# Expert weights of a sparse-attention and mixture-of-experts step: two of the six ring slots of an expert released half by half and loaded as halves of 1 MB

## What is computed

```python
logits = (x @ w_router) + b_router
top_v, top_e = lax.top_k(logits, 4)          # 4 of 32 experts for each row
gates = jax.nn.softmax(top_v, axis=-1)
...
gu = xe @ w_gu[e] + b_gu[e]                  # 1024 x 2048 weights
gate = jnp.minimum(gu[:, :1024], 7.0)
up = jnp.clip(gu[:, 1024:], -7.0, 7.0)
act = (up + 1.0) * gate * jax.nn.sigmoid(1.702 * gate)
y[rows] += gates[rows] * (act @ w_down[e] + b_down[e])   # 1024 x 1024 weights
...
y_prompt, y_sample = rms_norm(x + y, g_final)
```

## Time and profile before

| | us |
|---|---|
| median of 3 runs | 1653.48 |
| lowest, highest | 1653.24, 1654.1 |
| the profiled execution | 1653.29 |
| its span, first to last instruction | 1651.8 |
| TensorE matmuls busy | 1615.7 (98%) |
| VectorE, ScalarE, GpSimd busy | 609.4, 302.4, 204.7 |
| moved by DMA | 510.01 MB, 309 GB/s over the span |

### The profile page before, as it was taken

How to read it: one execution, slowest core, us unless ns; L and a number is a source line. 1 busy time by engine, 2 the same in 40 slices (tenths; PEclk the granted TensorE clock), 3 DMA queues, 4 the chain that set the end, 5 groups by cost and what they waited for, 6 DMA issues and landing times. The chain is left out here.

```text
span 1651.8 us, 33511 instructions
## 1 busy us (share of the span) xinstructions
PE 1615.7 (98%) x13818; PEld 763.7 (46%) x13818; DVE 609.4 (37%) x1186; ACT 302.4 (18%) x618; POOL 204.7 (12%) x267
## 2 busy tenths in 40 slices
PE   9999999999998999999999999999999999999996
PEld 7677587786745333333333333333333333333332
DVE  4359549403315333323233233323333233323333
ACT  1310120017112111112111211121111211111112
POOL 3624300015000010000000000000000000000000
PEclk9999999999998899999999999999999999999996
DMA  7456646621454699999999999999999999999963
GB/s 239 145 171 215 230 150 217 214 76 74 172 205 158 229 397 395 392 401 398 393 395 390 402 389 400 386 399 395 392 390 396 399 392 403 386 398 395 398 261 114
DMA packets 70505, 510.01 MB, mean 309 GB/s; under 512 B 11310, under 2 KB 11758, under 8 KB 45230
## 3 DMA queue, kind: packets, MB, share of 16 engines
q1 hardware_dynamic: 60070, 485.28, 74.0%
q0 software_dynamic: 10384, 24.06, 6.2%
HBM read 491.61 MB, written 22.37 MB: 311 GB/s over the span
## 5 line engine op out<-in xcount | busy, mean ns | idle before, releaser
L1209 PE MATMUL PS<-weight_ring,region_experts 128*32 128x512 f32 x6144 | 680.2, 594 | 2.6 <-issue 1.7
L1209 PEld LDWEIGHTS PS<-weight_ring,region_experts 128*32 128x32 f32 x6144 | 200.5, 110 | 413.3 <-issue 410.4
L1216 PE MATMUL PS<-weight_ring,act_turned 128*32 128x512 f32 x2048 | 232.2, 594 | 0.0
L834 PE MATMUL PS<-region_x,region_w 128*128 128x260 f32 (+1 forms) x928 | 209.4, 385 | 0.9 <-DVE region_x L1415 0.9
L834 PEld LDWEIGHTS PS<-region_x,region_w 128*128 128x128 f32 x928 | 175.2, 190 | 31.8 <-issue 3.4
L1536 DVE TENSOR_TENSOR region_experts<-region_experts,region_x 128x640 bf16<-128x640 f32 x33 | 27.2, 825 | 402.0 <-DMA region_experts<-b_gu 402.0
L1216 PEld LDWEIGHTS PS<-weight_ring,act_turned 128*32 128x32 f32 x2048 | 63.3, 110 | 137.7 <-issue 134.0
L616 POOL DMA_INDIRECT y_acc<-region_x,idx_i x32 | 46.9, 1465 | 641.5 <-issue 641.5
L1222 PE MATMUL PS<-weight_ring,act_turned 128*32 128x256 f32 x2048 | 122.2, 379 | 0.0
L1222 PEld LDWEIGHTS PS<-weight_ring,act_turned 128*32 128x32 f32 x2048 | 66.6, 110 | 71.2 <-issue 38.3
L600 POOL DMA_INDIRECT region_x<-h_rows,idx_i x33 | 33.5, 1014 | 431.8 <-DVE idx_i L1551 352.3
(11 more groups left out here) (266 smaller groups left out, 1301.8 us busy)
## 6 DMA issues: line engine op xcount, KB each, us to landing
weight_ring<-w_gu SPq DMA_DIRECT2D x128, 2048.0 KB, 13.8
weight_ring<-w_down SPq DMA_DIRECT2D x64, 2048.0 KB, 16.6
region_w<-w_mt SPq DMA_DIRECT2D x33, 512.0 KB, 4.4
weight_ring<-cache_kT SPq DMA_DIRECT2D x64, 256.0 KB, 4.0
weight_ring<-cache_v SPq DMA_DIRECT2D x64, 256.0 KB, 4.0
weight_ring<-w_out SPq DMA_DIRECT2D x2, 2048.0 KB, 10.7
weight_ring<-bias_strip SPq DMA_DIRECT2D x1, 2560.0 KB, 13.1
region_x<-xT SPq DMA_DIRECT2D x4, 536.0 KB, 7.0
```

The source lines that it names most:

```text
L834: mm = pe.matmul(PB[j % 2][:, a, 0:width], lhs(k), rhs(k)[:, width * a:width * a + width], start=(k == 0), stop=(k == nk - 1))
L1209: mm = pe.matmul(out[GRP * j:GRP * j + GRP], hTe[:, k, GRP * g:GRP * g + GRP], weights(c)[:, k, :], start=(k == 0), stop=(k == KD - 1))
L1216: pe.matmul(bank(3)[GRP * j:GRP * j + GRP], actT[:, k, GRP * g:GRP * g + GRP], w_dn[:, k, 512 * q:512 * q + 512], start=(k == 0), stop=(k ...
```

## The change

In the expert loop SyncE no longer loads c1 and c3 whole after round 3. The first halves of both (k = 0 to 3, 8 KB of each partition) are loaded once TensorE has done steps 0 to 3 of round 3, for which there is a new semaphore, `third_half`; the second halves are loaded after the round, as the whole slots were. Both halves of a slot count up the slot's semaphore, so TensorE waits for 32 per expert in place of 16. The loads of expert 0 ahead of the loop are cut in the same way, with nothing else between the halves. For the signal, TensorE's call of steps 0 to 5 of round 3 is split into 0 to 3 and 4 to 5.

```diff
@@ -288,7 +288,7 @@
         hTe_ready h_done hfT_ready hfT_taken hf_done idx_ready kidx_in kinew_set kvu late_in lgp_done lgs_done
         log_taken m_done m_ready mask_done mb_done mb_ready mq_done mxT_ready nmax_s og_ready om_done ones_set
         out_done po_step pool_done pool_may pool_pad proj_done psT_ready ps_norm pt_ready pt_taken ptz_done
-        pv_pair rank_ready relu_done rms_set round_done router_ready row_ms rsumT_ready rsum_set s_ready
+        pv_pair rank_ready relu_done rms_set round_done third_half router_ready row_ms rsumT_ready rsum_set s_ready
         sel_ready sidx_taken sig_done slot5_set slot_ready slots_moved small_in smask_done sq_done sq_sum
         ss_ready stT_in strip_in sums_ready turned unused_done up_full vnew_in vtail_out warm_set wblk_done
         wcol_in wiT_in wi_out wo0_in wo1_in wv_in xg_done xn_in xt_ready y_ready zero_late zero_rows zi_set
@@ -420,6 +420,12 @@
                     src = w_down[bass.ds(e, 1), c - 4].rearrange("a p x -> (a p) x")
                 sp.dma_start(W6[:, slot(c):slot(c + 1)], src).then_inc(r_full[c], 16)
 
+            def half_load(c, z, e):
+
+                src = w_gu[bass.ds(e, 1), c].rearrange("a p x -> (a p) x")
+                at = RING // 2 * z
+                sp.dma_start(W6[:, slot(c) + at:slot(c) + at + RING // 2], src[:, at:at + RING // 2]).then_inc(r_full[c], 16)
+
             def bias_load(e):
                 sp.dma_start(b_rows[0:P:GRP, :], b_gu[bass.ds(e, 1)].rearrange("a j x -> (a j) x")).then_inc(S["b_rows_in"], 16)
 
@@ -432,8 +438,11 @@
                 item(n)
             for t in range(NTILE):
                 sp.dma_start(xn(t)[0:TROWS[t]], xnat[t * P:t * P + TROWS[t]]).then_inc(S["xn_in"], 16)
-            for c in range(2, 6):
-                ring_load(c, 0)
+            ring_load(2, 0)
+            half_load(3, 0, 0)
+            half_load(3, 1, 0)
+            ring_load(4, 0)
+            ring_load(5, 0)
             sp.wait_ge(S["proj_done"], J_A + KD)
             sp.dma_start(gffn, g_ffn.partition_broadcast(P)).then_inc(S["late_in"], 16)
             sp.dma_start(gfin, g_final.partition_broadcast(P)).then_inc(S["late_in"], 16)
@@ -444,8 +453,9 @@
                 sp.dma_start(y_acc[t * P:t * P + TROWS[t]], xn(t)[0:TROWS[t]]).then_inc(S["acc_init"], 16)
                 sp.wait_ge(S["hf_done"], n + 1)
                 sp.dma_start(h_rows[t * P:t * P + TROWS[t]], hf(t)[0:TROWS[t]]).then_inc(S["acc_init"], 16)
-            for c in range(2):
-                ring_load(c, 0)
+            ring_load(0, 0)
+            half_load(1, 0, 0)
+            half_load(1, 1, 0)
             sp.wait_ge(S["acc_init"], 16 * 2 * NTILE)
             sp.wait_ge(S["hfT_ready"], NTILE)
             sp.dma_start(bd_sb[0:NE], b_down).then_inc(S["bd_in"], 16)
@@ -458,9 +468,12 @@
                     ring_load(0, e)
                     sp.wait_ge(S["round_done"], (b * NE + e - 1) * ROUNDS + 2)
                     ring_load(2, e)
+                    sp.wait_ge(S["third_half"], b * NE + e)
+                    half_load(1, 0, e)
+                    half_load(3, 0, e)
                     sp.wait_ge(S["round_done"], (b * NE + e - 1) * ROUNDS + 3)
-                    ring_load(1, e)
-                    ring_load(3, e)
+                    half_load(1, 1, e)
+                    half_load(3, 1, e)
                     sp.wait_ge(S["b_wide_done"], b * NE + e)
                     bias_load(e)
                     for c in range(2):
@@ -1209,6 +1222,7 @@
                         mm = pe.matmul(out[GRP * j:GRP * j + GRP], hTe[:, k, GRP * g:GRP * g + GRP], weights(c)[:, k, :], start=(k == 0), stop=(k == KD - 1))
                 if k == KD - 1:
                     mm.then_inc(S["round_done"], 1)
+                return mm
 
             def down_wide(ks):
                 for k in ks:
@@ -1237,15 +1251,16 @@
                         e = i * 2 + u
                         ne = b * NE + e
                         pe.wait_ge(r_full[0], (ne + 1) * 16)
-                        pe.wait_ge(r_full[1], (ne + 1) * 16)
+                        pe.wait_ge(r_full[1], (ne + 1) * 32)
                         pe.wait_ge(S["hTe_ready"], b * SELS + e + 1)
                         gu_round(bank(0), ((0, 0), (0, 1), (0, 2), (1, 2)))
                         pick(b * SELS + e + 2, e + 1, 1 - u)
                         pe.wait_ge(r_full[2], (ne + 1) * 16)
-                        pe.wait_ge(r_full[3], (ne + 1) * 16)
+                        pe.wait_ge(r_full[3], (ne + 1) * 32)
                         gu_round(bank(1), ((2, 0), (2, 1), (2, 2), (3, 2)))
                         rest = ((1, 0), (1, 1), (3, 0), (3, 1))
-                        gu_round(bank(2), rest, range(6))
+                        gu_round(bank(2), rest, range(4)).then_inc(S["third_half"], 1)
+                        gu_round(bank(2), rest, range(4, 6))
                         pe.wait_ge(S["act_full"], ne * 2 + 1)
                         for k in range(4):
                             mm = pe.transpose(bank(7, P, P * k), act_t[0][:, P * k:P * k + P], ident)
```

## The result

| us | before | changed |
|---|---|---|
| median | 1654.1 (5 runs) | 1663.54 (5 runs) |
| lowest, highest | 1653.24, 1656.89 | 1662.7, 1666.29 |
| the profiled execution | 1653.29 | 1662.7 |
| its span | 1651.8 | 1661.0 |

The ratio is 1.0056, 95% interval 1.0044 to 1.0068: 9.4 us, where the prediction had 2.75. The change does what it says, and its direction was forecast, but the time lies above the range's 1661.5. Timed again on another chip, the same kernel gave 1.0050 (1.0037 to 1.0063).

The account below looks back on a forecast made before the run. The prediction took a lagging DMA engine to bound the later experts. Earlier halves -2.5, order +2.45 and smaller rows +2.8 gave +2.75 us, a median of 1656.2 us; 8-in-10 range 1645.8 to 1661.5.

Parts of the forecast that it names:

- the laggard: One or a few DMA engines always behind; 33.67 us of work per later expert, against TensorE's 33.38.
- (d): TensorE's split matmul loop and added signal, SyncE's extra wait and two more issues: no time.
- (b): Queue order c1a, c3a, c1b, c3b: c1 whole one half later, +2.45 us once, not per expert.
- (c): Rows of 8 KB instead of 16 in halved slots: 0.09 us per expert, +2.8 us, bounds 0 and 12.
- (a): First halves of c1 and c3 issued about 4.2 us earlier: -2.5 us once, no time in loaded experts.
- rival 2: Gather of next expert's rows meets full engines: late, or loads slowed 0.3 us per expert; 1662 to 1664, chance 0.20.
- Rival 1: Early halves fill a hole in the loads, TensorE runs at 33.38: -8.0 us, 1645.5; chance 0.26 with half cases.
- Rival 3: Each of the two more DMAs per expert costs a 2.9 us start: 180 us in all; chance 0.02.
- Rival 4: Halves go out early but land no earlier; called the forecast itself in loaded experts, no separate chance.

Follow-up runs that it names:

- the quarters: Kernel before with c1 and c3 loaded in quarters of 512 KB (4 KB rows), all after round 3 in the old order: 1672.61 us, ratio 1.0109.
- late halves: Kernel before with c1 and c3 cut in halves, all issued after round 3 in the old order: 1658.75 us, ratio 1.0024; again 1656.93, 1.0011.

## Why the prediction was wrong, step by step

**Right: the laggard bounds the later experts.** Taking 6 KB from four engines brought them from 33.65 to 33.42 us; taking all the biases away, to 33.38. The gain left in better loading was put at 8 us; the loop without bias loads is 1033.4 - 1025.4 = 8.0 us shorter. The timed runs give only 4.5, so that the two eights are equal is in part luck. The trace's records of a slot's semaphore say the same as the bound, in increments that no row here shows: c2 of the kernel before has its first engines' shares at 1035.1, the fifteenth's at 1039.2, and the last at 1041.2. What the prediction did not see is where the laggard's extra work comes from: it never counts the bias load, and taking that away was enough to bring the loop to TensorE's pace.

**Right: (d), nothing on TensorE or SyncE.** No wait of theirs is new but that for the weights. The first halves are issued at 1035.46, 17.9 us after the expert's start at 1017.54, as said. The comparison ends at 1021.6, and the selection starts at 1024.55: the loads no longer bind it.

**Right: (b), the order, once.** c1b lands 7.5 us after c2, where 7.4 was said. The order cost 2.6 us timed and 3.4 by the loops, for 2.45, and all of it came within the first ten experts.

**Right in kind: (c), smaller rows.** +2.8 us were predicted; 3.5 and 1.2 were timed, 4.0 and 3.6 are the loops'. c2 to c3b takes 10.0 us for 9.9: 0.10 us per expert, where 0.09 was taken. An 8 KB packet takes 0.309 us, where the straight line had 0.312.

**Wrong: (a), the earlier halves, -2.5 us.** It was argued that the early issue gives the laggard time once and otherwise nothing. The head start was there: relative to the loop's start the last load of the first loaded expert, c5, lands 3.0 us earlier than before, in the next two 1.4 to 1.8 earlier. But it is given back: by the fifth expert it is level, and from there the stream falls behind by about 0.2 us per expert. Half of that is the cut. The other half is the early issue itself, which costs 0.11 to 0.15 us in each later expert (2.2 to 2.9 us in twenty). Net, (a) came out at +1.0 us by the loops (1041.1 and 1042.5 against 1040.8) and at some +2 to +4.6 by the timed runs: 3.5 us or more from the -2.5 in the sum. The steps as measured, in loop lengths (means, where there are two profiles): cut 1037.2 - 1033.4 = +3.8, order 1040.8 - 1037.2 = +3.6, early issue 1041.8 - 1040.8 = +1.0, together +8.4. The prediction had +2.8, +2.45 and -2.5; two were somewhat small, and the third had the wrong sign. That the direction came out right is owed to the first two.

What failed is the sentence "for the laggard this gives no time in a loaded expert". It treats the laggard's work per expert as a fixed amount, but its work grew by 0.11 to 0.15 us when the halves went out early, and most of that (0.08 to 0.12 us) came in the gather's stretch. The likely reason is that the work takes longer when the other engines are busy at the same time, so that the idle 14% beside the gather let the laggard run faster; the packets of one engine were not followed, so this reason is argued and not shown. It is rival 2 by its second clause, *"if the laggard loses that much per expert to fuller memory"*, without the first (the gather is not late). Its price of 0.3 us per expert is two to three times what was measured. Its 1662 to 1664 holds the measured 1663.54 partly by luck: half of the quarter of a microsecond that is lost is the cut, and by its own terms, 9.3 us on top of 2.45, it should have read 1665. It had a chance of 0.20, and the range stopped below it, at 1661.5, though the prediction says that the range takes in its lower part.

**Rival 1, the loads catch up: not so.** Apart from the head start no hole of the laggard's was filled; TensorE's matmuls wait for w_gu 21 times. **Rival 3, a start for each DMA: not so**, by the quarters. **Rival 4**, halves that go out early and land no earlier, is what one sees in a loaded expert.

**Left open:** by what means the gather's stretch gets longer when it is filled, and whether without a gather the early issue costs nothing at all; whether the same engine is the last one throughout (in the kernel with late halves the last is only 0.4 us behind the fifteenth); why 64 partitions load at half the rate; and what makes the bias load cheaper when GpSimd issues it.

## What to carry to other kernels

Where the DMA share is 1.00 and a slot still lands late, look for the engine that lands last and for what only it carries: small loads of a few rows (here 0.2% of the bytes, 0.4% of the time) belong on all 16 engines, and that was worth more here than any reordering tried. Issuing a load earlier helps a queue that runs dry; behind a backlog it gained a few microseconds once here and then lost more than that, a little in every expert. Pieces of a load cost something each even in a full queue (0.10 us per expert for halves of 4 MB, 0.42 for quarters), and loading the pieces of two slots in turn delays the slot that is needed first.

## What the runs showed of the hardware

- A load of 64 partitions with rows of 16 KB moved 209 GB/s where one of 128 partitions moves 438: its packets took 1.23 us in place of 0.615, at a DMA share of 0.98.
- A load of four rows of 6 KB is four packets of 0.24 us (median), one for each of four engines. Spread over sixteen rows it let an expert, bound by its loads, pass 0.23 us sooner.
- Uncut, in halves and in quarters, 4 MB took 9.89, 9.99 and 10.31 us in a full queue, as packets of 0.611, 0.309 and 0.159 us make it; the 2.9 us by which c1's landing in the earlier trace rows is over that of a full queue are not paid for each DMA.
- A gather of 0.26 MB by rows cost the loads 2.2 us per expert, against the 0.6 us that 0.26 MB take at 438 GB/s.
